# Prompt attention of a decoder step with two key-value heads on the two halves of the array

## The chip, the cores and the metric

The program runs on one core of one Trainium2 chip. It is one launch with no arithmetic on the host. The metric is the device time of a run in microseconds (us), as the median of several runs. The engines are TensorE (PE; its weight loads are PEld), VectorE (DVE), ScalarE (ACT), GpSimd (POOL) and SyncE (SP).

## The reference, cut to what matters

One layer of a decoder is applied to a prompt of 1024 tokens and to 64 sample tokens (8 sequences of 8). Everything is float32. The part that matters here is attention over the prompt. An indexer scores each key for each query, and each query keeps its best 256 keys:

```python
def _select_attend(q, qi, wi, ki_all, q_pos, gather_kv):
    ...
    score = jnp.where(admissible[None], score, -jnp.inf)
    _, sel = lax.top_k(score, topk)
    valid = sel <= q_pos[None, :, None]
    k_sel, v_sel = gather_kv(sel)
    qg = q.reshape(B, Tq, KV_HEADS, ATT_HEADS // KV_HEADS, HEAD_DIM).astype(jnp.float32)
    logits = jnp.einsum('bqhgd,bqkhd->bqhgk', qg, k_sel.astype(jnp.float32)) * (HEAD_DIM ** -0.5)
    logits = jnp.where(valid[:, :, None, None, :], logits, -jnp.inf)
    p = jax.nn.softmax(logits, axis=-1)
    o = jnp.einsum('bqhgk,bqkhd->bqhgd', p, v_sel.astype(jnp.float32))
```

There are eight query heads and four key-value heads of width 64, so two query heads share a key-value head. The other vectors that the layer needs are twelve chunks of 512 columns of an adaptive modulation, `silu(c) @ ada_w + ada_b`, for nine rows (one prompt, eight samples), and four more for the last norm.

## The kernel before, in words

The kernel runs eleven stages one after the other, with a barrier of all engines between them (`build`): modulation, projection (`norm_project`), rotary embedding, index, prompt attention, sample attention, HGRN2, output projection, routing, experts and the combination. Each stage writes out one instruction list per engine by hand. An engine takes its list in order, and waits on semaphores stand in the list. All tiles are views of one SBUF tensor (`arena`), and PSUM is eight banks (`banks`) of 128 × 512 f32.

The projection leaves all tokens in `z`, in tiles of 128 tokens: 512 query columns (eight heads of 64), 256 key columns, 256 value columns and the indexer's columns. ACT evicts each 128 × 512 result at L380; TensorE has six PSUM banks for them, so it can be ahead.

The index stage leaves, for each prompt tile i, a mask of 128 × 128(i+1) elements at `ACC_AT[i]` that is 0 for a kept key and −1e30 for another. In it DVE selects the best keys in rounds of an eight-fold maximum and a replacement (L1154 to L1158), last of all for the samples. TensorE works through projections of the recurrence and then through modulation chunks `ADA1` to `ADA2` (4 to 8), whose weights SP loads into two buffers of 2 MB (L947), one load per finished chunk. Chunks `ADA2` to `ADA3` (9 to 11) are done in prompt attention: SP loads them at L1247 to L1249, and TensorE puts one of their matmuls after each head of the first tiles (L1328, L1330).

Prompt attention goes through tiles i = 0 to 7 and the eight heads of each. Keys are transposed at L1314 into `kT`, 64 partitions per head, and queries at L1270 into `qT` (evicted by ACT at L1378). For a head, TensorE computes logits of 128 queries × 128(i+1) keys with 64 rows of the array (L1282). Two sets of two PSUM banks alternate. DVE scales them and adds the mask (L1348), and takes the row maximum in a second pass (L1351). ACT takes the exponential and its sum (L1396). TensorE transposes the result in blocks of 128 (L1294), ACT copies up to four blocks at a time back to SBUF (L1406), and TensorE multiplies each transposed block, which is the stationary operand, with 64 columns of values (L1305), accumulating in PSUM. DVE divides by the sums (L1359). In TensorE's list the transposes of head n−2 come first, then the logits of head n, then the weighing of head n−2.

In sample attention DVE reorders the 64 sample queries first (L1560). POOL's gathers of cached keys and values for the first sample are issued in prompt attention (L1210).

## Time and profile before

| what | us |
|---|---|
| three runs | 2767.02, 2760.20, 2749.53 |
| median of the runs | 2760.2 |
| the profiled execution, from its first to its last instruction | 2771.9 |
| TensorE busy | 2316.9 (84%) |
| VectorE busy | 1067.3 (39%) |
| ScalarE busy | 483.6 (17%) |
| GpSimd busy | 175.0 (6%) |

The profiled execution is one more execution beside the three that were timed; no time but its span is given for it. Busy times are sums over the whole span, and several engines are busy at once. The end of a matmul is modelled and matmuls overlap, so the time that one takes in a stream is read from the starts of two neighbours, not from its length. `banks<-arena 64*128 64x512 f32 x4` is a group of four instructions that read `arena` and write `banks`: 64 rows and 128 columns of stationary operand, and a moving operand of 64 partitions × 512 columns. `[idle <-X]` is the engine's idle time before it, and what ended it. PEclk is the clock that TensorE was granted: 1.00 is 2.4 GHz, 0.50 is 1.2 GHz.

### The profile page before, as it was taken

To read this page: it belongs to the slowest core of one execution; us is meant where nothing else is said; L and a number is where in the kernel's file an instruction comes from. 1 tells how busy PE (TensorE), PEld (TensorE's weight loads), DVE (VectorE), ACT (ScalarE), POOL (GpSimd) and SP (SyncE) were. 2 spreads that over 40 slices of the span, in tenths; PEclk is the share of its full clock that TensorE was granted. 3 is DMA by queue.
4 is the path that set the end of the run, shared out by engine and by line. 5 is a ranking of instruction groups with operands and counts; after the bars stand their busy time and mean duration, and the time that the engine had idled before them with its cause. 6 is when DMAs were issued, how large, how long until landed. Compare 5 with 4: busy or idle time off the path is not lost. (4 is left out here: it accounts for less than half of the span.)

```text
span 2771.9 us, 20892 instructions
## 1 busy us (share of the span) xinstructions
PE 2316.9 (84%) x6937; PEld 1125.3 (41%) x6938; DVE 1067.3 (39%) x2104; ACT 483.6 (17%) x832; POOL 175.0 (6%) x153
## 2 busy tenths in 40 slices
PE   5999799899991789999999579779668999999950
PEld 1444444244420346666333135435334444444420
DVE  1300469999999132222221443333411111001128
ACT  1100156210000232222111421011100000000012
POOL 0000025100000000000000000000000000000024
PEclk8999855599995575555999665589779999999985
DMA  7100210111140200001332530052178843843343
GB/s 255 58 4 0 89 45 0 46 51 66 67 143 22 100 32 1 0 1 63 137 137 92 195 112 1 4 194 91 44 274 317 314 154 141 289 165 136 136 161 112
DMA packets 117117, 294.57 MB, mean 106 GB/s; under 512 B 14862, under 2 KB 22286, under 8 KB 114483
## 3 DMA queue, kind: packets, MB, share of 16 engines
q1 hardware_dynamic: 98020, 200.90, 20.8%
q0 software_dynamic: 14272, 75.77, 7.3%
q10 hardware_dynamic: 4752, 16.93, 1.6%
q8 instruction: 46, 0.75, 0.1%
q14 instruction: 27, 0.22, 0.0%
HBM read 312.01 MB, written 44.35 MB: 129 GB/s over the span
## 5 line engine op out<-in xcount | busy, mean ns | idle before, releaser
L2066 PE MATMUL banks<-arena 128*128 x832 | 368.7, 602 | 17.2 <-DMA arena<-in_w 15.8
L1069 PE MATMUL banks<-arena 128*128 128x512 f32 (+3 forms) x656 | 255.8, 552 | 3.7 <-DMA arena<-in_ada_w 3.7
L2066 PEld LDWEIGHTS banks<-arena 128*128 128x128 f32 x832 | 159.7, 193 | 223.3 <-issue 223.3
L1154 DVE MAX8 arena<-arena 128x8 f32<-128x384 f32 (+3 forms) x224 | 238.6, 1083 | 12.9 <-DVE arena L1158 12.5
L1158 DVE MATCH_REPLACE8 arena<-arena 128x384 f32<-128x384 f32 (+3 forms) x224 | 240.7, 1075 | 0.0
L2130 DVE TENSOR_TENSOR arena<-arena,banks 128x512 f32<-128x512 f32 x26 | 17.9, 687 | 538.1 <-PE banks L2066 375.6
L364 PE MATMUL banks<-arena 128*128 128x512 f32 (+3 forms) x576 | 204.2, 515 | 0.0
L2080 PE MATMUL banks<-arena 128*128 x416 | 185.4, 599 | 11.3 <-DVE arena L2134 11.3
L1069 PEld LDWEIGHTS banks<-arena 128*128 128x128 f32 (+2 forms) x656 | 107.8, 177 | 150.8 <-issue 144.2
L1348 DVE SCALAR_TENSOR_TENSOR arena<-banks,arena 128x128 f32<-128x128 f32 (+7 forms) x64 | 48.5, 758 | 282.7 <-PE banks L1282 282.7
L1305 PEld LDWEIGHTS banks<-arena 128*128 128x128 f32 x576 | 117.0, 304 | 59.2 <-issue 38.3
L1305 PE MATMUL banks<-arena 128*128 128x64 f32 x576 | 128.3, 401 | 13.1 <-ACT arena L1406 13.1
L364 PEld LDWEIGHTS banks<-arena 128*128 128x128 f32 (+1 forms) x576 | 94.6, 186 | 104.6 <-issue 104.5
L1282 PE MATMUL banks<-arena 64*128 64x512 f32 (+3 forms) x192 | 134.9, 836 | 0.0
L1002 PE MATMUL banks<-arena 64*128 64x512 f32 (+3 forms) x192 | 127.1, 854 | 4.4 <-ACT arena L1090 2.8
L1736 PE MATMUL banks<-arena 128*128 128x512 f32 (+1 forms) x288 | 127.0, 600 | 2.8 <-DMA arena<-in_w_out 2.8
L2080 PEld LDWEIGHTS banks<-arena 128*128 128x128 f32 x416 | 77.0, 190 | 104.2 <-issue 104.2
L2107 ACT ACTIVATE arena<-banks 128x1024 f32<-128x1024 f32 x26 | 26.6, 1023 | 411.3 <-PE banks L2080 411.3
L1002 PEld LDWEIGHTS banks<-arena 64*128 64x128 f32 x192 | 58.3, 326 | 69.0 <-issue 55.7
L1396 ACT ACTIVATE arena<-arena 128x128 f32<-128x128 f32 (+7 forms) x64 | 49.4, 773 | 186.3 <-DVE arena L1351 186.2
L1736 PEld LDWEIGHTS banks<-arena 128*128 128x128 f32 (+1 forms) x288 | 53.0, 187 | 70.4 <-issue 69.8
L1282 PEld LDWEIGHTS banks<-arena 64*128 64x128 f32 x192 | 50.2, 297 | 77.2 <-issue 77.2
(352 smaller groups left out, 2485.8 us busy)
## 6 DMA issues: line engine op xcount, KB each, us to landing
arena<-in_w SPq DMA_DIRECT2D x78, 2048.0 KB
arena<-in_ada_w SPq DMA_DIRECT2D x9, 2048.0 KB, 8.5
tmp_yslot<-arena ACTq DMA_DIRECT2D x32, 512.0 KB, 2.8
arena<-in_w_in SPq DMA_DIRECT2D x7, 2048.0 KB, 8.6
arena<-in_ada_final_w SPq DMA_DIRECT2D x4, 2048.0 KB
arena<-in_ada_w SPq DMA_DIRECT2D x3, 1792.0 KB
arena<-in_x_prompt SPq DMA_DIRECT2D x1, 4096.0 KB, 25.3
arena<-in_w_out SPq DMA_DIRECT2D x2, 2048.0 KB
```

The costliest lines, as they stand in the source:

```text
L364: ins = pe.matmul(ps[0:r, n % NBK, 0:wd], hT[:, a, i * P:i * P + r], w[j % 3][:, a, 0:wd], start=(a == 0), stop=(a == KD - 1))
L1002: ins = pe.matmul(ps[:, b + c // 512, 0:w], qiT[:, h, :], kiT[:, c:c + w], start=True, stop=True)
L1069: ins = pe.matmul(ps[0:m, PB[n % 4], 0:cols], lhs(a), rhs(a), start=(a == 0), stop=(a == KD - 1 and j < len(chunks)))
L1154: ve.max(top[u][0:acc.shape[0], :], acc).then_inc(s["top"], 1)
L1158: ve.match_replace(acc, top[u][0:acc.shape[0], :], acc, TAKEN).then_inc(s["top"], 1)
L1282: ins = pe.matmul(ps[:, b + c // 512, 0:w], qT[i % 2][:, h, :], kT[:, h // 2, c:c + w], start=True, stop=True)
L1305: ins = pe.matmul(ps[:, 6 + i % 2, h * HD:(h + 1) * HD], PT[m % 4][:, u, :], z[:, c + u, VC + (h // 2) * HD:VC + (h // 2 + 1) * HD], start ...
L1348: ve.scalar_tensor_tensor(L[n % 2][:, 0:N], ps[:, b:b + 2, :].rearrange("p a b -> p (a b)")[:, 0:N], float(HD) ** -0.5, ar.view(ACC_AT[i], ...
L1396: act.activation(E[m % 2][:, 0:N], L[m % 2][:, 0:N], ACT.Exp, bias=nmx[:, m:m + 1], accum_out=den[:, m:m + 1]).then_inc(s["e"], 1)
L1736: ins = pe.matmul(ps[0:r, OUT[n % 3], :], mT[i % 2][:, a, 0:r], wo[:, a, c * 512:(c + 1) * 512], start=(a == 0), stop=(a == KD - 1))
L2066: ins = pe.matmul(ps[:, 2 + m, :], XT[b][:, a, :], w(m * 4096 + a * FE, FE), start=(a == 0), stop=(a == KD - 1))
L2080: ins = pe.matmul(ps[:, 5 + c, :], hT[:, a, :], w(8192 + a * D + c * 512, 512), start=(a == 0), stop=(a == 3))
```

## The change

Prompt attention is written anew. Tiles go from i = 7 down to 0, and each has two groups g of four query heads (two key-value heads 2g and 2g+1, two query heads r each).

- Keys and queries of two key-value heads (a = 0, 1) lie on partitions 0 to 63 and 64 to 127. Each transpose is 128 columns wide (16 for the keys, four per tile for the queries), and the logits of the two heads are matmuls on the two row halves of the array, into different banks. To make the queries of a pair neighbours, the projection's eviction of the query columns reorders heads, in two instructions of 256 columns in place of one of 512, and the sample stage's reordering reads that order.
- The scale goes into the eviction of the queries. One DVE instruction adds the mask, negates, and keeps the row minimum. ACT takes the exponential in place, with scale −1.
- The transposes are done per block c of 128 keys for the four heads of a group (four transposes into one bank). ACT copies the even blocks and DVE the odd ones.
- The values (64 columns) are the stationary operand on one column half of the array per key-value head, and 256 columns of transposed weights are moving. The output comes out transposed: DVE copies it to SBUF, TensorE turns it back, and DVE divides by the sums.
- For tiles of more than 512 keys one call of logits (r) takes all four logits banks, so it waits for the masks of the call before. TensorE's order in step n is: logits (n, 0), first half of the blocks of group n−1, logits (n, 1), second half.
- `ADA2` is 12: the three chunks of modulation are done at the end of the index stage, and SP has nothing to do in prompt attention.

The diff, with the added lines of `prompt_attention` that matter (most of the removed ones are in the listing above and are left out):

```diff
-ADA2, ADA3 = 9, 12
+ADA2, ADA3 = 12, 12
...
-                act.activation(z[0:r, i, c:c + wd], ps[0:r, n % NBK, 0:wd], ACT.Copy).then_inc(s["ev"], 1)
+                if j == 0:
+                    for g in range(2):
+                        w = slice(256 * g, 256 * g + 256)
+                        ins = act.activation(z[0:r, i, w].rearrange("p (r a d) -> p a r d", a=2, d=HD), ps[0:r, n % NBK, w].rearrange("p (a r d) -> p a r d", r=2, d=HD), ACT.Copy)
+                    ins.then_inc(s["ev"], 1)
+                else:
+                    act.activation(z[0:r, i, c:c + wd], ps[0:r, n % NBK, 0:wd], ACT.Copy).then_inc(s["ev"], 1)
...
+    A = ar.view(O_A, NT, 512)
+    kT = ar.view(O_KT, 2, SEQ)
+    PT = [ar.view(O_KT + 2 * SEQ + b * 512, 512) for b in range(4)]
...
+    LE = [ar.view(o + b * 2 * SEQ, 2, SEQ) for b in range(4)]; o += 8 * SEQ
+    qT = [ar.view(o + b * 512, 4, P) for b in range(2)]; o += 1024
...
+    order = [NT - 2 - j for j in range(NT - 1)]
+    groups = [(j, i, g) for j, i in enumerate(order) for g in range(2)]
+    base = [0]
+    for j, i, g in groups:
+        base.append(base[-1] + i + 1)
+    NG = len(groups)
+    wide = [P * (i + 1) > 512 for _, i, _ in groups]
+    def out_t(j, i):
+        return z[:, i, QC:QC + 512]
+    def halves(n):
+        i = groups[n][1]
+        return (range(0, (i + 2) // 2), range((i + 2) // 2, i + 1))
...
+            def logits(n, r):
+                j, i, g = groups[n]
+                q, N = 2 * n + r, P * (i + 1)
+                if g == 0 and r == 0:
+                    pe.wait_ge(s["ev"], j + 1)
+                first_narrow = not wide[n] and r == 0 and n > 0 and wide[n - 1]
+                if wide[n] or first_narrow:
+                    pe.wait_ge(s["l"], 2 * q)
+                elif q >= 2:
+                    pe.wait_ge(s["l"], 2 * (q - 1))
+                b = 0 if wide[n] else q % 2
                 for c in range(0, N, 512):
                     w = min(512, N - c)
+                    for a in range(2):
+                        rs = slice(HD * a, HD * a + HD)
+                        ins = pe.matmul(ps[:, 2 * a + b + c // 512, 0:w], qT[j % 2][rs, 2 * g + r, :], kT[rs, g, c:c + w], start=True, stop=True)
                 ins.then_inc(s["mm"], 1)
+            def turn(n, c):
+                m = base[n] + c
+                if c == 0:
+                    pe.wait_ge(s["e"], 4 * (n + 1))
+                if m >= 2:
+                    pe.wait_ge(s["pta"] if m % 2 == 0 else s["ptd"], m // 2)
+                for u in range(4):
+                    a, r = divmod(u, 2)
+                    ins = pe.transpose(ps[:, 4 + m % 2, u * P:(u + 1) * P], LE[(2 * n + r) % 4][:, a, c * P:(c + 1) * P], k.ident)
+                ins.then_inc(s["pt"], 1)
+            def weigh(n, c):
+                j, i, g = groups[n]
+                m = base[n] + c
+                if c == 0 and n >= 1:
+                    pe.wait_ge(s["oc"], n)
+                pe.wait_ge(s["pta"] if m % 2 == 0 else s["ptd"], m // 2 + 1)
+                for a in range(2):
+                    v0 = VC + (2 * g + a) * HD
+                    ins = pe.matmul(ps[HD * a:HD * a + HD, 6, 0:256], z[:, c, v0:v0 + HD], PT[m % 4][:, 256 * a:256 * a + 256], start=(c == 0), stop=(c == i))
                 ins.then_inc(s["pv"], 1)
+            def blocks(n, cs):
+                i = groups[n][1]
+                for c in cs:
+                    if c == 0:
+                        turn(n, 0)
+                    if c < i:
+                        turn(n, c + 1)
+                    weigh(n, c)
...
+            for b in range(4):
+                for v in range(2):
+                    for g in range(2):
+                        ins = pe.transpose(ps[:, b, (2 * v + g) * P:(2 * v + g + 1) * P], z[:, 2 * b + v, KC + g * P:KC + (g + 1) * P], k.ident)
+            pe.wait_ge(s["kc"], 4)
+            for n in range(NG + 1):
+                j, g = divmod(n, 2)
+                if g == 1 and j >= 1:
+                    turn_out(j - 1)
+                if n < NG:
+                    logits(n, 0)
+                if g == 1 and j + 1 < NT - 1:
+                    queries(j + 1)
+                if n >= 1:
+                    blocks(n - 1, halves(n - 1)[0])
+                if n < NG:
+                    logits(n, 1)
+                if n >= 1:
+                    blocks(n - 1, halves(n - 1)[1])
+            turn_out(NT - 2)
         @block.vector
...
+            def mask(n, r, a):
+                j, i, g = groups[n]
+                q, N = 2 * n + r, P * (i + 1)
+                if a == 0:
+                    ve.wait_ge(s["mm"], q + 1)
+                    if n >= 2:
+                        ve.wait_ge(s["pt"], base[n - 1])
+                b = 0 if wide[n] else q % 2
+                col = H * i + 4 * g + 2 * a + r
+                ve.tensor_tensor_reduce(LE[q % 4][:, a, 0:N], ps[:, 2 * a:2 * a + 2, :].rearrange("p a b -> p (a b)")[:, b * 512:b * 512 + N],
+                                        ar.view(ACC_AT[i], N), -1.0, 3.0e38, ALU.add, ALU.min, nmx[:, col:col + 1]).then_inc(s["l"], 1)
+            def copy_turned(n, cs):
+                for c in cs:
+                    m = base[n] + c
+                    if m % 2 == 0:
+                        continue
+                    ve.wait_ge(s["pt"], m + 1)
+                    if m >= 4:
+                        ve.wait_ge(s["pv"], m - 3)
+                    ve.tensor_copy(PT[m % 4], ps[:, 4 + m % 2, :]).then_inc(s["ptd"], 1)
+            def copy_out(n):
+                j, i, g = groups[n]
+                ve.wait_ge(s["pv"], base[n + 1])
+                ve.tensor_copy(out_t(j, i)[:, 256 * g:256 * g + 256], ps[:, 6, 0:256]).then_inc(s["oc"], 1)
+            def out(j):
+                i = order[j]
+                cols = slice(H * i, H * i + H)
+                ve.reciprocal(rden[:, cols], den[:, cols]).then_inc(s["rd"], 1)
+                ve.wait_ge(s["rd"], j + 1)
+                ve.wait_ge(s["ot"], j + 1)
+                for g in range(2):
+                    w = slice(256 * g, 256 * g + 256)
+                    ins = ve.tensor_tensor(A[:, i, w].rearrange("p (a r d) -> p a r d", r=2, d=HD), ps[:, 7, w].rearrange("p (r a d) -> p a r d", a=2, d=HD),
+                                           rden[:, H * i + 4 * g:H * i + 4 * g + 4].rearrange("p (a r) -> p a r", r=2).unsqueeze(3).broadcast_to([P, 2, 2, HD]), ALU.mult)
+                ins.then_inc(s["o"], 1)
+            for b in range(4):
+                ve.wait_ge(s["ks"], b + 1)
+                ve.tensor_copy(kT[:, :, 2 * b * P:(2 * b + 2) * P].rearrange("p g (v c) -> p g v c", c=P),
+                               ps[:, b, :].rearrange("p (v g c) -> p g v c", g=2, c=P)).then_inc(s["kc"], 1)
+            for n in range(NG + 1):
+                j, g = divmod(n, 2)
+                if g == 1 and j >= 1:
+                    out(j - 1)
+                for r in range(2):
+                    cs = halves(n - 1)[r] if n >= 1 else range(0)
+                    if n < NG:
+                        mask(n, r, 0)
+                    copy_turned(n - 1, cs[0:len(cs) // 2])
+                    if n < NG:
+                        mask(n, r, 1)
+                    copy_turned(n - 1, cs[len(cs) // 2:])
+                if n >= 1:
+                    copy_out(n - 1)
+            out(NT - 2)
         @block.scalar
...
+            def queries(j):
+                act.wait_ge(s["tr"], j + 1)
+                if j >= 2:
+                    act.wait_ge(s["mm"], 4 * (j - 1))
+                act.activation(qT[j % 2].rearrange("p a b -> p (a b)"), ps[:, 7, :], ACT.Copy, scale=float(HD) ** -0.5).then_inc(s["ev"], 1)
+            def expo(n, r):
+                j, i, g = groups[n]
+                q, N = 2 * n + r, P * (i + 1)
+                for a in range(2):
+                    col = H * i + 4 * g + 2 * a + r
+                    act.wait_ge(s["l"], 2 * q + a + 1)
+                    act.activation(LE[q % 4][:, a, 0:N], LE[q % 4][:, a, 0:N], ACT.Exp, bias=nmx[:, col:col + 1], scale=-1.0, accum_out=den[:, col:col + 1]).then_inc(s["e"], 1)
+            def copy_turned(n, cs):
+                for c in cs:
+                    m = base[n] + c
+                    if m % 2:
+                        continue
+                    act.wait_ge(s["pt"], m + 1)
+                    if m >= 4:
+                        act.wait_ge(s["pv"], m - 3)
+                    act.activation(PT[m % 4], ps[:, 4 + m % 2, :], ACT.Copy).then_inc(s["pta"], 1)
+            for n in range(NG + 1):
+                j, g = divmod(n, 2)
+                if n >= 1:
+                    expo(n - 1, 1)
+                if g == 1 and j + 1 < NT - 1:
+                    queries(j + 1)
+                if n >= 1:
+                    copy_turned(n - 1, halves(n - 1)[0])
+                if n < NG:
+                    expo(n, 0)
+                if n >= 1:
+                    copy_turned(n - 1, halves(n - 1)[1])
...
-                               .rearrange("p (c g d) -> p g c d", g=2, d=HD)).then_inc(s["qr"], 1)
+                               .rearrange("p (g c d) -> p g c d", g=2, d=HD)).then_inc(s["qr"], 1)
```

## Rows read from the trace of the kernel before

**Rows 1.** The page's head.

```profile
span 2771.9 us, 20892 instructions
```

**Rows 2.** Windows: start:end, length; per engine busy us (instructions); clock; DMA share, GB/s.

```profile
842.00:894.60 52.60, 0.00 (x0) 0.00 (x0) 50.79 (x50) 0.00 (x0) 0.00 (x0) 0.50 0.00 0
895.60:900.20 4.60, 4.58 (x22) 3.84 (x23) 2.83 (x5) 0.00 (x0) 1.88 (x2) 0.50 0.72 235
900.20:907.00 6.80, 3.33 (x25) 2.48 (x23) 3.44 (x8) 3.62 (x8) 0.00 (x0) 1.00 1.05 436
895.60:1299.60 404.00, 370.11 (x1206) 228.13 (x1206) 108.30 (x152) 108.66 (x244) 1.88 (x2) 0.57 0.07 27
1023.10:1292.70 269.60, 260.19 (x815) 176.42 (x815) 72.95 (x79) 74.19 (x148) 0.00 (x0) 0.50 0.00 0
1309.80:1347.00 37.20, 37.20 (x120) 12.42 (x119) 8.52 (x7) 5.17 (x10) 0.94 (x1) 1.00 0.23 87
```

**Rows 3.** Timeline of one head of i=7: start us, length us, instructions.

```profile
1245.73 1.92 PE L1294 MATMUL banks<-arena 128*128 128x128 f32 x8
...
1246.83 0.60 ACT L1406 ACTIVATE arena<-banks 128x512 f32<-128x512 f32 x1 [0.70 <-PE banks L1294]
...
1247.57 3.78 PE L1282 MATMUL banks<-arena 64*128 64x512 f32 x4
...
1251.28 3.67 PE L1305 MATMUL banks<-arena 128*128 128x64 f32 x16
1251.39 1.23 DVE L1348 SCALAR_TENSOR_TENSOR arena<-banks,arena 128x1024 f32<-128x1024 f32 x1 [5.71 <-PE banks L1282]
...
1253.90 1.15 ACT L1396 ACTIVATE arena<-arena 128x1024 f32<-128x1024 f32 x1 [5.63 <-DVE arena L1351]
...
1254.75 0.42 PE L1294 MATMUL banks<-arena 128*128 128x128 f32 x1
```

**Rows 4.** Groups by line within prompt attention, 895.6 to 1299.6.

```profile
L1348 DVE SCALAR_TENSOR_TENSOR arena<-banks,arena 128x128 f32<-128x128 f32 (+7 forms) x64 | 48.5, 758 | 282.7 <-PE banks L1282 282.7
...
L1328 PE MATMUL banks<-arena 128*9 128x512 f32 x48 | 35.5, 834 | 11.3 <-DMA arena<-in_ada_b 11.3
```

**Rows 5.** Timeline of TensorE in the index stage, the last two chunks of modulation.

```profile
823.42 7.04 PE L1069 MATMUL banks<-arena 128*9 128x512 f32 x16 [1.26 <-DMA arena<-in_ada_w]
...
832.46 7.04 PE L1069 MATMUL banks<-arena 128*9 128x512 f32 x16 [1.05 <-DMA arena<-in_ada_w]
```

**Rows 6.** Groups by line over the whole span, VectorE and ScalarE.

```profile
L380 ACT ACTIVATE arena<-banks 128x512 f32<-128x512 f32 (+3 forms) x36 | 18.2, 505 | 181.5 <-PE banks L364 181.5
L2134 DVE COPY arena<-banks 128x512 f32<-128x512 f32 x26 | 18.0, 691 | 19.5 <-PE banks L2072 19.5
...
L641 DVE TENSOR_TENSOR_SCAN arena<-arena 128x1088 f32<-128x1088 f32 x4 | 9.7, 2416 | 0.0
```

**Rows 7.** Timeline of the sample stage, transposes and weighing on two column halves.

```profile
1355.84 0.66 PE L1518 MATMUL banks<-arena 128*128 128x128 f32 x4
...
1356.42 2.86 PE L1534 MATMUL banks<-arena 128*64 128x256 f32 x16
...
1359.21 0.66 PE L1518 MATMUL banks<-arena 128*128 128x128 f32 x4
```

**Rows 8.** Timeline of the sample stage, two weight loads, 512-column passes.

```profile
1313.70 0.14 PEld L1497 LDWEIGHTS banks<-arena 128*64 128x64 f32 x1 [0.29 <-issue]
1314.13 0.14 PEld L1497 LDWEIGHTS banks<-arena 128*64 128x64 f32 x1 [0.29 <-issue]
```

**Rows 9.** Timeline of TensorE in the index stage, two row halves, then one.

```profile
520.96 1.97 PE L1025 MATMUL banks<-arena 64*64 64x512 f32 x4 [0.69 <-ACT arena L1100]
522.72 3.62 PE L1008 MATMUL banks<-arena 64*64 64x512 f32 x4
```

**Rows 10.** Timeline of the stage's last instructions and the next stage's first.

```profile
1295.76 2.00 PE L1305 MATMUL banks<-arena 128*128 128x64 f32 x16 [0.25 <-ACT arena L1406]
...
1299.60 0.52 SPq L1439 DMA_DIRECT2D arena<-k_rsel  x1
```

More of the change, by code:

```diff
@@ L1230, in prompt_attention @@
[L1230 to L1252 removed]
+    assert o <= O_K0, (o, O_K0)
@@ L1298, in weigh @@
-            def weigh(i, h):
-                m = first[i, h]
-                if h == 0:
-                    pe.wait_ge(s["ev"], 2 * i + 2)
-                for c in range(0, i + 1, 4):
-                    pe.wait_ge(s["ptc"], m + 1)
-                    for u in range(min(4, i + 1 - c)):
-                        ins = pe.matmul(ps[:, 6 + i % 2, h * HD:(h + 1) * HD], PT[m % 4][:, u, :], z[:, c + u, VC + (h // 2) * HD:VC + (h // 2 + 1) * HD],
-                                        start=(c + u == 0), stop=(c + u == i))
-                    m += 1
-                ins.then_inc(s["pv"], 1)
@@ new lines, in blocks, with turn_out @@
+            def blocks(n, cs):
[6 more added lines that the diff above has]
+                    weigh(n, c)
+            def turn_out(j):
+                i = order[j]
+                pe.wait_ge(s["oc"], 2 * j + 2)
+                pe.wait_ge(s["ev"], min(j + 2, NT - 1))
+                for u in range(4):
+                    ins = pe.transpose(ps[:, 7, u * P:(u + 1) * P], out_t(j, i)[:, u * P:(u + 1) * P], k.ident)
+                ins.then_inc(s["ot"], 1)
@@ L1315, in _ @@
+            for b in range(4):
+                for v in range(2):
+                    for g in range(2):
+                        ins = pe.transpose(ps[:, b, (2 * v + g) * P:(2 * v + g + 1) * P], z[:, 2 * b + v, KC + g * P:KC + (g + 1) * P], k.ident)
                 ins.then_inc(s["ks"], 1)
             queries(0)
-            pe.wait_ge(s["kc"], NT - 1)
-            for n in range(H * (NT - 1) + 2):
-                i, h = divmod(n, H)
-                if n >= 2:
-                    turn(*divmod(n - 2, H))
-                chunk, u = divmod(n - 2, ADA_EVERY)
-                if n >= 2 and chunk < len(ada) and u < KD:
-                    if u == 0:
-                        pe.wait_ge(s["aw"], 48 * (chunk + 1))
-                        if chunk:
-                            pe.wait_ge(s["ae"], chunk)
-                    pe.matmul(ps[0:NC, 1, :], k.cT[:, u, :], wa[:, u, :] if u < KD - 1 else wb, start=(u == 0), stop=False)
-                    if u == KD - 1:
-                        pe.matmul(ps[0:NC, 1, :], k.ones, bias, start=False, stop=True).then_inc(s["ap"], 1)
-                if n == 4 * H:
-                    pe.wait_ge(s["ae"], len(ada))
-                if n < H * (NT - 1):
-                    logits(i, h)
-                    if h == 4 and i + 1 < NT - 1:
-                        queries(i + 1)
-                if n >= 2:
-                    weigh(*divmod(n - 2, H))
@@ new lines, in out @@
+            def out(j):
+                i = order[j]
+                cols = slice(H * i, H * i + H)
[7 more added lines that the diff above has]
+                ins.then_inc(s["o"], 1)
```

132 lines of the change are left out of this document (10 added, 122 removed).

## The prediction

> **What bounds the kernel now.** I read the page's head first [rows 1], then busy time and granted clock in windows, because the share of the whole span (PE 84%) says nothing about one stage. Prompt attention is the stretch from 895.6 to 1299.6: 404.0 us, PE busy 370.1, DVE 108.3, ACT 108.7, clock 0.57 on average [rows 2]. So TensorE bounds it, and mostly at its lower level: from 1023.1 to 1292.7 it is busy 260.2 of 269.6 us at 0.50 (1.2 GHz) [rows 2]. Next I read the timeline of one late head (i=7) [rows 3], from start to start: eight transposes take 1.84 us (1245.73 to 1247.57), four passes of logits 3.71, sixteen passes of weighing 3.47; 9.02 us, and the next head follows without a gap. An f32 matmul is two instructions (four for the two calls of L1282, [rows 3]); a transpose is one. The logits fill 64 of the array's 128 rows and cost 0.85 us per 512 columns and pass. The weighing streams only 64 columns per pass, yet a pass takes 3.47/16 = 0.217 us, as long as a 128-column transpose (0.21): it pays for loading 128 stationary columns. Nothing here waits for DVE or ACT; DVE waits 282.7 us for logits [rows 4].
>
> **The chunks of modulation that move.** Three chunks leave the stage (PE 35.5 us busy and 11.3 us of waits, [rows 4]) for the end of the index stage. There each costs 9.04 us from start to start, its load included (823.42 to 832.46, [rows 5]), so 27 us after 841.5, until about 869. The index stage ends only with DVE's selection: from 842.0 to 894.6 PE is idle and DVE busy 50.8 of 52.6 [rows 2]. I cost them at nothing; without that cover they would be 27. Three more loads, bias loads and row stores go to SP's queue there, which nothing else needs until the barrier. In the projection nine evictions become eighteen smaller ones; ACT waited 181.5 us for PE at that line [rows 6], so nothing. The sample stage reads the same bytes in another order: nothing. POOL's gathers stay.
>
> **The new attention, at full clock.** The unit is a block: 128 keys for the four heads of a group; 2 groups × 36 = 72 blocks.
> - Transposes of a block: four, 0.58 us with the change of array mode before the next matmul (1355.84 to 1356.42, [rows 7]).
> - Weighing: two column halves, two passes each, 256 columns. Do halves overlap? In the sample stage sixteen such passes, eight on either half, take 2.79 us (1356.42 to 1359.21, [rows 7]). A 512-column pass at full clock is 0.43 (1313.70 to 1314.13, [rows 8]), so 256 columns are 0.215, and sixteen in a row would be 3.44. They overlap, though the order of issue there (eight, then eight) gives it only half a chance. Here halves alternate after two passes: 2 slots = 0.43, plus the 0.21 that 2.79 holds beyond 12 slots: 0.64. A block is 1.22 us, 72 are **87.8**.
> - Logits: row halves. In the index stage four passes on two row halves take 1.76 us at half clock (520.96 to 522.72, [rows 9]), where four on one half take 3.71 [rows 3]: full overlap. The 32 calls stream 4 × 128 × 36 = 18432 columns, 36 times 512, in two slots of 0.43: 31.0; with 0.30 per call for entering and leaving the row mode (3.71 − 4 × 0.85, [rows 3]) 9.6 more: **40.6**.
> - Queries in and outputs back: 16 sets of four transposes at 0.58, **9.3**.
>
> Is it hidden? One group of i=7 by hand: PE has two calls (4.0) and eight blocks (9.8), 13.8 us. DVE has four masks of 1.23 if the new pass costs what the masking pass costs now [rows 3], four copies of 0.69 and one of at most that [rows 6]: 8.4. ACT has four exponentials of 1.15 and four copies of 0.60 [rows 3]: 7.0, and the reads of four sums. A copy starts about 0.3 us after the last transpose, lasts 0.60 or 0.69, and PE has the weighing of the block before and the next transposes, 1.22, to cover it. It fails where DVE has just begun a mask (up to 1.2 us, about once per half group), where ACT does the last two exponentials before the next group's turn (narrow tiles), and eight times where turning the output back waits for the copy-out (0.75). I take **28** in all (6 for the last, 22 for the others), between 0 and 60. In narrow groups (i below 2) ACT's own 3 to 4 us per group hold the pace.
>
> The unseen operation is the mask with its minimum. From below it is the present masking pass, 48.5 us for 64 [rows 4]; from above two cycles per element, as the scan takes (2.42 us for 1088 elements, [rows 6]), 97. Masking and plain copies of 1024 take 1.22 to 1.23, and less is excluded, since it reads as many elements, so I take 48.5. DVE's second pass goes, which nothing waited for but ACT's exponential.
>
> Start: sixteen key transposes, copies, then three calls and two rounds of masks before the first block, because a wide tile holds all four banks of logits: 17 us, 11 beside the calls counted above. Until the clock rises these cost some **8** more. End: copy, turn, scale, barrier, **5** (now 1295.76 to 1299.60, [rows 10]).
>
> Sum: 87.8 + 40.6 + 9.3 + 28 + 11 + 8 + 5 = **190 us** against 404: 214 saved. The profiled span is 2771.9 [rows 1] and would be 2558; that execution stands 11.7 above the median of the three runs, so I put **2546**.
>
> **Does the clock rise?** It stayed at 0.50 through 269.6 us of heads with logits on one row half, PE busy 260.2. It was 1.00 after 4.6 us of nothing but key transposes at the stage's start, PE busy 4.58, and held 1.00 in the sample stage with its mix of transposes and column halves [rows 2]. With logits on both row halves, everything left resembles those. The Trainium skill, "TensorE: Matmul & The Clock Gate", Part 4 (PE-mode transpose), speaks against it: transposes don't count as activity for the clock, which would lead to the first rival below. The start of this stage disagrees: only key transposes ran, and the clock went to 1.00 [rows 2].
>
> **The rivals.**
> - *Half clock stays.* For it: the present stage. Block 0.99 + 1.11 = 2.1 × 72 = 151; logits 36 × 1.71 + 32 × 0.31 = 71; sets 16; waits 14; start 16; end 5: 273, so **2629**. Chance 0.11.
> - *Halves overlap only across their border, in strict order of issue*: two passes on the first half, two on the second make three slots, not two. Weighing 72 × 0.215 = 15.5, logits one slot per call (0.27 on average narrow, 0.43 wide) 11: **2573**. Against it: 1.76 us for four passes is two slots, not three [rows 9]. Chance 0.07. The Trainium skill, "TensorE: Matmul & The Clock Gate", Part 3 (What overlaps and what doesn't), states this strict order of matmuls; the trace disagrees, by those 1.76 us.
> - *DVE becomes the bound.* Masks at 97: DVE 97 + 24.8 (36 copies of 0.69) + 11 (16 copies out, at most 0.69) + 10 (scaling, eight times two of half a bank) + 3 (keys) + 10 (gaps) = 156, in one queue with copies that PE waits for; about 1 us more per half group, 32: **2578**. For it: each weighing waits for a copy. Chance 0.09.
> - *Halves don't overlap in this order*: 31 + 31 at full clock, **2608**; at half clock stage 396, **2752**, no change. Chance 0.04, half each.
> - *Slower: a chain through the four logits banks.* PE's next call waits for both masks, the copies stand behind masks and exponentials, and every step runs alone at half clock: blocks 72 × (1.0 + 0.95 + 1.1) = 220; 32 calls × (2.2 + 1.8 masks + 2.1 exponentials) = 195; rest 45: 460, **2816**. It decides when copies regularly stand behind an exponential whose logits PE issues after the weighing that needs the copy; the order written here puts them ahead. Chance 0.02.
>
> **How the numbers follow.** The forecast has 0.67. Its low end is no waits and full clock at once (154, 2510), with the run spread (2749.5 to 2767.0) 2505. Upwards 2610 takes in the strict order, DVE's two cycles and the serial halves at full clock; outside are half clock, the rest of serial halves, the slower case and the forecast's own tails, 0.2. A measurement tells about 1% (28 us) from no change. Faster 0.96, same 0.02, slower 0.02.
>
> **What would show it.** Stage length near 190; clock 1.00 from some 15 us after its start; masks of 1.23 for 1024; two matmuls on opposite halves starting together; index ending as before. A stage above 240 at full clock means that waits were mis-sized, at 0.50 that the clock was; an index stage that ends later means that the chunks were not covered.

## The result and the profile after

The changed kernel takes **2540.62 us** (median of four runs, 2538.1 to 2545.16), the kernel before, run beside it, 2763.61; the ratio is 0.918, with a 95% interval of 0.9134 to 0.9227. The forecast was 2546; how much of that hit is luck is said further down. The profiled execution is one of 2541.94 us with a span of 2539.8, against the span in [rows 1].

First the windows of the changed kernel. The columns are those of [rows 2]: start and end, length, busy time of PE, PEld, DVE, ACT and POOL with their instructions, mean granted clock, DMA share, GB/s. The first row is the end of the index stage, the next four are prompt attention in pieces, the last is all of it.

```profile
842.00:897.70 55.70, 45.94 (x104) 8.33 (x102) 53.82 (x55) 3.52 (x6) 0.00 (x0) 0.98 0.56 191
898.70:919.60 20.90, 15.19 (x56) 8.97 (x56) 8.76 (x14) 7.84 (x12) 1.88 (x2) 0.67 0.50 201
919.60:929.90 10.30, 9.91 (x63) 4.78 (x64) 6.19 (x10) 5.74 (x10) 0.00 (x0) 1.00 0.00 0
929.90:1059.60 129.70, 109.03 (x696) 57.52 (x692) 64.85 (x161) 59.92 (x139) 0.00 (x0) 0.99 0.00 1
1059.60:1074.90 15.30, 8.40 (x40) 4.42 (x36) 5.66 (x23) 3.12 (x13) 0.00 (x0) 0.60 0.00 1
898.70:1074.90 176.20, 142.53 (x848) 75.70 (x848) 85.46 (x208) 76.62 (x173) 1.88 (x2) 0.92 0.06 25
```

Prompt attention took 404.0 us [rows 2] and takes 176.2. That is 227.8 of the 232.1 us by which the span fell; the rest is small and of both signs. PE works 142.5 us instead of 370.1, and its clock is 0.92 on average instead of 0.57. It is 1.00 from 919.3 to 1049.0 and stands at 0.50 at times at the two ends: in the first 21 us and in the last 26, where the tiles are narrow.

The groups by line in this stretch (busy us, mean ns of one, then idle time before them and who ended it) answer to [rows 4]:

```profile
L1425 ACT ACTIVATE arena<-arena 128x1024 f32<-128x1024 f32 (+7 forms) x64 | 48.9, 767 | 17.9 <-DVE arena L1361 17.9
L1307 PE MATMUL banks<-arena 128*64 128x256 f32 x288 | 47.5, 409 | 19.8 <-DVE arena L1372 15.3 <-ACT arena L1435 4.4
L1361 DVE CUSTOM_DVE_ANT_0 arena<-banks,arena 128x1024 f32<-128x1024 f32 (+7 forms) x64 | 46.8, 754 | 59.6 <-PE banks L1285 59.6
...
L1361 DVE DVE_READ_ACCUMULATOR2_ANT arena<- 128x1 f32 x64 | 5.3, 83 | 0.0
```

L1361 is the mask with its minimum. It costs 46.8 us and 5.3 for reading the minima, so it runs at the speed of the old masking pass, 48.5 for 64 [rows 4], and not at the 97 us that the prediction had as its upper end. PE's waits in the stage, from the view of waits (total, times, longest):

```profile
PE banks L1307 <- DVE arena L1372: 15.3, 21, 1.5
PE banks L1285 <- DVE arena L1361: 4.9, 2, 2.5
PE banks L1307 <- ACT arena L1435: 4.4, 11, 0.8
PE banks L1324 <- DVE arena L1377: 4.2, 8, 0.5
PE banks L1296 <- ACT arena L1425: 2.1, 2, 1.3
```

Weighing (L1307) waits mostly for DVE's copies of transposed blocks (L1372), 21 times. The timeline of TensorE at full clock shows the unit of the sum, a block (tile i=6), and two of the waits:

```profile
939.76 0.65 PE L1307 MATMUL banks<-arena 128*64 128x256 f32 x4
940.35 0.66 PE L1296 MATMUL banks<-arena 128*128 128x128 f32 x4
941.05 0.65 PE L1307 MATMUL banks<-arena 128*64 128x256 f32 x4
941.63 0.66 PE L1296 MATMUL banks<-arena 128*128 128x128 f32 x4
942.22 0.65 PE L1307 MATMUL banks<-arena 128*64 128x256 f32 x4
943.07 0.65 PE L1307 MATMUL banks<-arena 128*64 128x256 f32 x4 [0.20 <-DVE arena L1372]
944.25 0.66 PE L1324 MATMUL banks<-arena 128*128 128x128 f32 x4 [0.53 <-DVE arena L1377]
944.84 1.77 PE L1285 MATMUL banks<-arena 64*128 64x512 f32 x8
946.54 0.66 PE L1267 MATMUL banks<-arena 128*128 128x128 f32 x4
```

From start to start: weighing 0.58 (941.05 to 941.63), transposes 0.59 (941.63 to 942.22), a block 1.17. The logits call for 896 keys takes 1.70 us (944.84 to 946.54). Its passes are two of 512 and two of 384 columns for each of two heads; one after the other, at 0.43 per 512 [rows 8], they would be 2.99.

### The profile page after: what moved, and what is told of

It is laid out like the page before. It is cut to its first block and busy times, and to the rows that moved or that the text cites. A ratio compares the mean times of both kernels' runs of the same rounds, so it can differ in the third digit from the quotient of the medians.

```text
span 2539.8 us, 20125 instructions
## 1 busy us (share of the span) xinstructions
PE 2135.9 (84%) x6633; PEld 982.0 (39%) x6634; DVE 1045.7 (41%) x2160; ACT 454.1 (18%) x773; POOL 175.4 (7%) x153
## 5 line engine op out<-in xcount | busy, mean ns | idle before, releaser
L1075 PE MATMUL banks<-arena 128*128 128x512 f32 (+3 forms) x704 | 277.0, 555 | 4.7 <-DMA arena<-in_ada_w 4.6
L2108 PEld LDWEIGHTS banks<-arena 128*128 128x128 f32 x832 | 158.5, 192 | 219.7 <-issue 219.7
L364 PE MATMUL banks<-arena 128*128 128x512 f32 (+3 forms) x576 | 203.9, 514 | 0.0
L1008 PE MATMUL banks<-arena 64*128 64x512 f32 (+3 forms) x192 | 127.1, 854 | 2.7 <-ACT arena L1088 1.5
L2122 PEld LDWEIGHTS banks<-arena 128*128 128x128 f32 x416 | 76.9, 190 | 104.4 <-issue 104.4
L1008 PEld LDWEIGHTS banks<-arena 64*128 64x128 f32 x192 | 58.2, 326 | 67.4 <-issue 54.1
L1778 PEld LDWEIGHTS banks<-arena 128*128 128x128 f32 (+1 forms) x288 | 53.1, 187 | 70.6 <-issue 70.5
L1625 DVE COPY arena<-banks 128x1024 f32<-128x1024 f32 x32 | 38.9, 1223 | 91.2 <-PE banks L1527 91.2
L1138 ACT ACTIVATE arena<-banks 128x512 f32<-128x512 f32 (+3 forms) x44 | 23.9, 544 | 265.6 <-PE banks L1075 200.2
L1361 DVE CUSTOM_DVE_ANT_0 arena<-banks,arena 128x1024 f32<-128x1024 f32 (+7 forms) x64 | 46.8, 754 | 59.6 <-PE banks L1285 59.6
L1539 PE MATMUL banks<-arena 128*64 128x512 f32 x128 | 63.0, 615 | 5.7 <-DVE arena L1625 5.7
L540 PE MATMUL banks<-arena 128*9 128x512 f32 x64 | 36.3, 730 | 36.8 <-DMA arena<-in_ada_final_w 36.8
```

What stands on the lines that cost most here:

```text
L364: ins = pe.matmul(ps[0:r, n % NBK, 0:wd], hT[:, a, i * P:i * P + r], w[j % 3][:, a, 0:wd], start=(a == 0), stop=(a == KD - 1))
L540: pe.matmul(ps[0:NC, 4 + n, :], k.cT[:, a, :], wa[n % 2][:, a, :], start=(a == 0), stop=False)
L1008: ins = pe.matmul(ps[:, b + c // 512, 0:w], qiT[:, h, :], kiT[:, c:c + w], start=True, stop=True)
L1075: ins = pe.matmul(ps[0:m, PB[n % 4], 0:cols], lhs(a), rhs(a), start=(a == 0), stop=(a == KD - 1 and j < len(chunks)))
L1361: ve.tensor_tensor_reduce(LE[q % 4][:, a, 0:N], ps[:, 2 * a:2 * a + 2, :].rearrange("p a b -> p (a b)")[:, b * 512:b * 512 + N], ar.view(A ...
L1539: pe.matmul(out, QB[:, b, pp, :], kT[(4 * b + c) % 2][:, pp, :], start=(pp == 0), stop=False)
```

## The experiments

The stage in the table is prompt attention in the profiled run, cut at its first and last instruction (403.2 us before, 175.7 changed, so cut). Where "after" stands under base, the edit is made to the changed kernel.

| kernel | base | time, us | ratio to before, 95% | stage, us |
|---|---|---|---|---|
| e1: chunks moved, nothing else | before | 2748.36 | 0.9903 to 0.9953 | 380.0 |
| e2: e1, logits on 128 rows | before | 2604.05 | 0.9383 to 0.9431 | 236.7 |
| e8: mask and minimum in one pass | before | 2771.27 | 0.9993 to 1.0034 | 414.0 |
| e3: logits on 128 rows | after | 2573.27 | 0.9274 to 0.9320 | 208.2 |
| e11: other order of passes | after | 2539.09 | 0.9118 to 0.9244 | 175.0 |
| e5: no column halves | after | 2561.83 | 0.9239 to 0.9271 | 193.1 |
| e4: two passes on DVE | after | 2586.27 | 0.9334 to 0.9364 | 220.4 |
| e6a: a copy ahead of the masks | after | 2531.24 | 0.9132 to 0.9164 | 166.1 |
| e6b: e6a, turning between halves | after | 2523.73 | 0.9099 to 0.9131 | 158.1 |
| e9: e6b, blocks in pairs | after | 2520.64 | 0.9092 to 0.9143 | 156.0 |
| e7: e6b, tile 3 first | after | 2521.88 | 0.9094 to 0.9145 | 159.1 |

**e1**: the chunks alone.

```diff
-ADA2, ADA3 = 9, 12
+ADA2, ADA3 = 12, 12
...
```

> The kernel before, with the three chunks moved to the index stage and nothing else (the heads stay one by one, on 64 rows, with two passes for mask and maximum). My theory: moving the chunks is a small part of the gain. The stage of 404 us loses their 35.5 + 4.8 + 11.3 us of TensorE work and waits, but the two stretches at a granted clock of 1.00, in which the chunks' matmuls ran beside the heads, may go with them, and at 0.50 they would cost about 44 us more: 20 to 47 us off, 2715 to 2740 us in all. Rival, that the move is what counts (the rest of the rewriting only moves work about): the stage falls towards 190, and the time below 2600 us.

The time falls by 20 us of 2768, at the small end of the 20 to 47 that were expected; 2748 itself lies above the range of 2715 to 2740. Windows of the kernel before, in the two stretches of heads that ran at 1.00, with chunks among them, then of e1:

```profile
965.00:988.90 23.90, 21.04 (x94) 9.61 (x94) 8.89 (x18) 8.97 (x26) 0.00 (x0) 1.00 0.02 3
1002.60:1023.10 20.50, 18.84 (x83) 8.65 (x82) 8.80 (x14) 6.33 (x15) 0.00 (x0) 1.00 0.00 1
```

```profile
899.60:906.40 6.80, 4.23 (x29) 3.17 (x28) 3.83 (x10) 3.69 (x9) 0.00 (x0) 0.98 1.01 434
906.40:1274.80 368.40, 349.69 (x1102) 234.52 (x1102) 101.48 (x138) 104.14 (x233) 0.00 (x0) 0.50 0.01 2
```

The stage is 23 us shorter and 368 us of it now run at 0.50. So those two stretches did go with the chunks, and the move is a tenth of the gain.

**e2**: the same, with logits that fill the array's rows. Each query is padded with zeros, so half of the multiplications are by zero.

```diff
-    kT, A = ar.view(O_KT, HKV, SEQ, p=HD), ar.view(O_A, NT, 512)
+    kT, A = ar.view(O_KT, 2, SEQ), ar.view(O_A, NT, 512)
...
-    ins = pe.matmul(ps[:, b + c // 512, 0:w], qT[i % 2][:, h, :], kT[:, h // 2, c:c + w], ...)
+    ins = pe.matmul(ps[:, b + c // 512, 0:w], qT[i % 2][:, h, :], kT[:, h // 4, c:c + w], ...)
...
```

> e1 with the logits on all 128 rows: each head's query is padded with 64 rows of zeros and meets the keys of two kv heads. The passes stay as many and as wide as in e1, nothing overlaps, and mask and maximum stay two passes. Theory A, that half of the gain is the granted clock, which stays at 0.50 while the array is fed on 64 rows: the stage runs at 1.00 and falls from about 370 to 190 to 210 us, 2540 to 2590 us in all. Theory B, that the clock rises only with what else is new (two halves at once, no gap between the steps): the clock stays at 0.50 and the time as e1's, about 2725 us.

Theory A holds: 144 us less than e1, with as many passes and columns of logits. Windows of e2, the stage in two pieces:

```profile
894.80:920.10 25.30, 18.45 (x73) 14.81 (x74) 9.99 (x34) 9.51 (x32) 1.89 (x2) 0.50 0.42 166
920.10:1131.50 211.40, 180.26 (x1065) 134.29 (x1063) 97.91 (x127) 96.72 (x225) 0.00 (x0) 0.94 0.00 1
```

It was 14 us slower than theory A's upper end. A mean of 0.94 over 211.4 us is 25 us at 0.50, and the first 25.3 us run at 0.50 too: together at most some 25 us lost to the clock, which the expectation had left out. The edit also spares the changes of mode around a call. At the 0.3 us that the prediction has for a call [rows 3] they are some 20 us for 64 calls at half clock, an estimate and a small part of the 144, and the changed kernel, which has them, runs at 1.00.

**e8**: the one pass on DVE alone.

```diff
-    ve.scalar_tensor_tensor(L[n % 2][:, 0:N], ..., ALU.mult, ALU.add).then_inc(s["l"], 1)
-    ve.wait_ge(s["l"], n + 1)
-    ve.tensor_reduce(nmx[:, n:n + 1], L[n % 2][:, 0:N], AX.X, ALU.max, negate=True).then_inc(s["mx"], 1)
+    ve.tensor_tensor_reduce(L[n % 2][:, 0:N], ..., -1.0, 3.0e38, ALU.add, ALU.min, nmx[:, n:n + 1]).then_inc(s["l"], 1)
...
```

> The kernel before, with mask and minimum in one pass on VectorE and nothing else (the chunks stay, the heads stay one by one). My theory: VectorE is not the bound, it waits 282.7 us for logits in this stage, so no change: 2755 to 2764 us. Rival, that the second pass lay in the chain from head to head: 64 reductions of 0.3 to 1.1 us go, 20 to 45 us off, 2715 to 2740 us.

No change against the kernel before in the same set of runs (2768.43), as expected, though 2771 is above the range that was written down: DVE falls from 108.3 us busy [rows 2] to 60.8 in the stage, and nothing comes of it. The stage's 414.0 in the table comes from the longest of the ten runs, in which the mean clock of the stage was 0.55, against 0.57 [rows 2].

**e3**: the changed kernel without overlap of the row halves.

```diff
-    ins = pe.matmul(..., qT[j % 2][rs, 2 * g + r, :], kT[rs, g, c:c + w], ...)
+    ins = pe.matmul(..., qT[j % 2][:, a, u * P:(u + 1) * P], kT[:, g, c:c + w], ...)
...
```

> The changed kernel with queries padded by 64 rows of zeros, so that each logits matmul has all 128 rows: the two row halves no longer run at once, everything else stays. Theory A, that passes on the two row halves overlap and save 4 slots of 0.427 us in a call of 8 passes: half of the slots come back, 72 slots of 0.427 us, +31 us, 2565 to 2578 us. Rival B, that the passes don't overlap or TensorE waits for others anyway, and what the two kv heads bring is the clock alone: 2538 to 2548 us as the changed kernel.

Theory A: 33 us slower, the stage 32.5 longer. The logits, from start to start and less their waits, take 30 us more (71.4 against 41.7), and all of PE's waits in the stage 7 more (39.2 against 31.8). A call on 1024 keys takes 3.54 us in e3 (timeline of TensorE at full clock, start to start), eight passes of 0.43 in a row:

```profile
928.17 3.70 PE L1285 MATMUL banks<-arena 128*128 128x512 f32 x8
931.71 0.60 PE L1296 MATMUL banks<-arena 128*128 128x128 f32 x4
```

**e11**: the passes of a call, sorted by head.

```diff
-    for c in range(0, N, 512):
-        for a in range(2):
+    for a in range(2):
+        for c in range(0, N, 512):
```

> The changed kernel with the passes of a logits call in another order: both column pieces of one kv head, then both of the other, instead of the two heads in turn. Nothing else is changed; all logits stay on 64 rows. Theory A, that passes on the two row halves overlap only with their neighbour in the queue, and that the clock falls when TensorE works on 64 rows for longer: of 72 saved slots some 60 come back (a call of 8 passes takes 7 slots instead of 4), 26 us at full clock, and half-clock stretches appear in the middle of the stage for 10 to 40 us more, 2571 to 2586 us. Theory B, that only the overlap is lost and the clock stays: 2563 to 2570 us. Theory C, that the halves overlap in any order: 2538 to 2546 us.

Theory C: the time is that of the changed kernel. The same call of 896 keys takes 1.71 us in e11's timeline:

```profile
931.90 1.78 PE L1285 MATMUL banks<-arena 64*128 64x512 f32 x8
933.61 0.66 PE L1296 MATMUL banks<-arena 128*128 128x128 f32 x4
```

In the trace its eight passes start in four pairs, the first at 931.90 and 931.91. So the two halves run beside each other in either order of issue, and the rival of strict order is out. The clock stays at 1.00 from 913.2 to 1049.7.

**e5**: the weighing without column halves.

```diff
-    for a in range(2):
-        v0 = VC + (2 * g + a) * HD
-        ins = pe.matmul(ps[HD * a:HD * a + HD, 6, 0:256], z[:, c, v0:v0 + HD], PT[m % 4][:, 256 * a:256 * a + 256], ...)
+    v0 = VC + 2 * g * HD
+    pe.matmul(ps[:, 6, :], z[:, c, v0:v0 + P], PT[m % 4], ...).then_inc(s["pv"], 1)
...
```

> The changed kernel without the two column halves in the weighing: the values of both heads stand on 128 columns and all 512 probability columns pass, so that half of the products are not used, and there is no change of mode between the transposes and the weighing. Theory A, that a block pays 0.30 us for its two changes of mode and saves one slot of 0.427 us by the two halves running at once: +0.13 us for each of 72 blocks, +9 us, 2546 to 2554 us. Rival B, that the changes of mode cost nothing: +0.427 us for each, +31 us, 2565 to 2577 us. Rival C, that the halves don't run at once: -0.30 us for each, 2515 to 2525 us.

The time, 21 us longer (the stage 17.4), lies between A and B. The prices hold for an undisturbed step, and the count was wrong. TensorE's timeline in e5:

```profile
937.87 1.02 PE L1306 MATMUL banks<-arena 128*128 128x512 f32 x2
938.73 0.60 PE L1296 MATMUL banks<-arena 128*128 128x128 f32 x4
...
948.83 0.60 PE L1296 MATMUL banks<-arena 128*128 128x128 f32 x4
949.26 1.02 PE L1306 MATMUL banks<-arena 128*128 128x512 f32 x2
```

Four transposes take 0.43 us here (948.83 to 949.26) and 0.585 in the changed kernel; an undisturbed weighing takes 0.86 (937.87 to 938.73) and 0.58. So a step that ends in a change of mode pays 0.15 us for it: the changed kernel's weighing is one slot of 0.43 and 0.15, where e5's is two slots, and the overlap saves 0.43. But a block doesn't have two changes within the group: the last two weighings of a group follow each other, and logits lie between the halves. In the changed kernel's trace the order of TensorE's instructions goes from transposes to weighing 58 times and back 32 times. So 72 × 0.427 − 90 × 0.15 = 17 us, close to the stage's 17.4. In part that is luck: transposes and weighing, less their waits, take 19 us more in e5 (106.3 against 87.0), and the rest of the stage is shorter, as it stood at 0.50 for 12 us in e5 and for 29 in the changed kernel.

**e4**: the changed kernel with mask and maximum in two passes.

```diff
-    ve.tensor_tensor_reduce(LE[q % 4][:, a, 0:N], ..., -1.0, 3.0e38, ALU.add, ALU.min, nmx[:, col:col + 1]).then_inc(s["l"], 1)
+    ve.scalar_tensor_tensor(LE[q % 4][:, a, 0:N], ..., ALU.mult, ALU.add).then_inc(s["l"], 1)
+    ve.wait_ge(s["l"], 2 * q + a + 1)
+    ve.tensor_reduce(nmx[:, col:col + 1], LE[q % 4][:, a, 0:N], AX.X, ALU.max, negate=True).then_inc(s["mx"], 1)
...
```

> The changed kernel with mask and maximum in two passes on VectorE again (64 reductions come back, a wait between the passes). Theory A, that VectorE, at 85.5 of 176.2 us busy but in the chain from logits to exponentials and to the copies of transposed blocks, has no room for 48 us more in one piece: a half's copies come later by up to 1.1 us, TensorE waits, +15 to +35 us, 2555 to 2576 us. Rival B, that VectorE has slack (TensorE is busy 142.5 of 176.2 us): no change, 2538 to 2546 us.

Theory A's mechanism, but 46 us, more than its upper end. Waits of e4, then two windows, the second just after a fall of the clock, and the wait in front of that fall:

```profile
PE banks L1307 <- DVE arena L1374: 36.7, 27, 3.3
PE banks L1285 <- DVE arena L1361: 7.4, 2, 3.7
```

```profile
920.90:1101.80 180.90, 137.57 (x763) 71.24 (x761) 111.85 (x177) 69.45 (x153) 0.00 (x0) 0.88 0.00 1
965.30:972.10 6.80, 5.83 (x21) 3.02 (x22) 2.29 (x4) 1.13 (x2) 0.00 (x0) 0.50 0.00 0
```

```profile
966.27 1.97 PE L1307 MATMUL banks<-arena 128*64 128x256 f32 x8 [3.27 <-DVE arena L1374]
```

PE's waits within the stage grow from 31.8 to 55.8 us, some 24 more. And the clock is 0.88 over the middle, 43 us at half speed, where the changed kernel has 3. Each of the nine falls in the middle follows a wait of 1.7 to 3.3 us; two waits of 1.8 us were followed by none. At half speed TensorE loses at most half of the added 48 us (76 against 29 over the whole stage, from the mean clocks of its windows), another 24. The two are enough for the 45 us by which the stage grew; no run here has the waits without the fall of the clock.

**e6a and e6b**: which waits of the changed kernel can go. e6a lets DVE and ACT copy the first block of a half's second half before that half's masks and exponentials; e6b moves the outputs' and the next queries' transposes, with their copies and scaling, between the halves.

```diff
+    def copies(n):
+        i = groups[n][1]
+        cut = min((i + 2) // 2 + 1, i + 1)
+        return (range(0, cut), range(cut, i + 1))
...
-                    cs = halves(n - 1)[r] if n >= 1 else range(0)
+                    cs = copies(n - 1)[r] if n >= 1 else range(0)
...
```

```diff
-                if g == 1 and j >= 1:
-                    turn_out(j - 1)
                 if n < NG:
                     logits(n, 0)
-                if g == 1 and j + 1 < NT - 1:
-                    queries(j + 1)
                 if n >= 1:
                     blocks(n - 1, halves(n - 1)[0])
+                if g == 1 and j >= 1:
+                    turn_out(j - 1)
                 if n < NG:
                     logits(n, 1)
+                if g == 1 and j + 1 < NT - 1:
+                    queries(j + 1)
...
```

> The changed kernel with the copy of the first transposed block of a half's second half moved ahead of that half's masks on VectorE (and its counterpart on ScalarE ahead of the exponentials). My theory: in the trace of the changed kernel the first block of the second half takes 1.3 to 1.74 us instead of 1.2, since its copy waits behind a mask that itself waits for the next logits: some 0.5 us in 14 groups go, -4 to -10 us, 2531 to 2537 us. Rival: the wait only moves to the next block or to the mask, and so to the exponentials: 2538 to 2546 us.

> e6a, and besides the transposes of the outputs and of the next queries moved off the ends of a group to between its two halves, on all three engines. My theory: the 8 waits of about 0.6 us before an output's transposes for the copy-out of its sum on VectorE find other work in front of them, -5 us against e6a: 2525 to 2533 us. Rival: these waits are covered by what follows or come back at the next block: as e6a, 2531 to 2537 us, or as the changed kernel.

My theory holds for both: 2531.24 us, and 2523.73, 1.3 below the range and 0.7% below the changed kernel. The stage falls by 9.6 and by 8.0 more. Waits of e6a, then of e6b:

```profile
PE banks L1312 <- DVE arena L1377: 6.0, 13, 0.9
...
PE banks L1329 <- DVE arena L1382: 4.3, 8, 0.6
```

```profile
PE banks L1312 <- DVE arena L1377: 5.4, 12, 0.9
PE banks L1290 <- DVE arena L1366: 4.9, 2, 2.5
...
PE banks L1312 <- ACT arena L1440: 4.3, 12, 0.8
PE banks L1301 <- ACT arena L1430: 3.3, 5, 1.6
```

The 15.3 us for copied blocks fall to 6.0; the eight waits before an output's transposes, 4.3 us, are gone from e6b but for one of 0.5. That is half of e6b's 8.0. The rest goes with the clock: it stood at 0.50 for 11 us of the stage in e6b and for 23 in e6a (29 in the changed kernel), most of it at the start, where the two clocks part before the first instruction that e6b moves, so I don't put it down to the edit.

**e9 and e7**, both on e6b: blocks in pairs, with the copies of two blocks instead of one ahead of a half's masks and exponentials, and tile 3 first.

```diff
+                for p in range(0, len(cs), 2):
+                    pair = cs[p:p + 2]
+                    for c in pair:
+                        if c + 2 <= i:
+                            turn(n, c + 2)
+                    for c in pair:
+                        weigh(n, c)
...
```

```diff
-    order = [NT - 2 - j for j in range(NT - 1)]
+    order = [3, 7, 6, 5, 4, 2, 1, 0]
```

> e6b with the blocks of a half taken in pairs: two blocks' transposes, then two blocks' weighings, where it was one and one. My theory: a change between transposes and weighing costs 0.15 us of TensorE (e5's rows: 0.437 and 0.861 us for the four transposes and the weighing without a change, 0.585 and 0.583 with one), and about 40 of the 90 changes inside the groups go: -6 us, -8 to -3, 2515 to 2521 us. Rival: the copies of a pair come closer together and fall behind the masks and exponentials, so that the waits of 9.7 us for copied blocks grow by as much: 2522 to 2530 us.

> e6b with another order of the query tiles: tile 3 (512 keys) first, then 7, 6, 5, 4, 2, 1, 0. My theory: the first block's transposes start 16.8 us after the stage begins, with two waits of 2.5 us for masks on 1024 keys; masks half as long and two buffers for the logits of 512 keys take these waits away and let the first block begin some 3 us earlier, also at the half clock: -1 to -6 us, 2518 to 2523 us. Rival: the wait goes to the change from 512 to 1024 keys, where the logits wait for all masks: 2523 to 2527 us.

Neither can be told from e6b by its time. In e9 transposes and weighing together take 88.3 us of TensorE's start times instead of 95.4, the 7 us that were meant, but the first logits ran longer at 0.50 (until 917.9, in e6b until 913.4) and the logits took 4.7 more. That start need not be the edit's: in e6a, too, the clock rose for good only 22.7 us after the stage's start, as in e9, and 18.8 in e6b. In e6a and e9 TensorE had stood idle for 52 us before the stage, in e6b for 4.6. In e7 the first transposes begin 11.4 us after the stage's start, in e6b 16.8 (timeline of TensorE):

```profile
896.95 3.65 PE L1335 MATMUL banks<-arena 128*128 128x128 f32 x16 [52.52 <-PEq L138]
...
908.35 1.10 PE L1301 MATMUL banks<-arena 128*128 128x128 f32 x8 [1.38 <-ACT arena L1430]
```

The stage is none the shorter for it, 159.1 against 158.1 us, so my theory falls although the time lies in its range. Part of the 5 us went into an end at 0.50, from 1049.4 on (6.7 us, in e6b 2.8); over the whole stage it stood at 0.50 for 19 us, in e6b for 11, which can cost 4 us at most. The wait that the rival named is not among TensorE's waits, and where the rest went is open.

## Why the prediction held, by its steps

The terms against the changed kernel's trace, each TensorE instruction counted from its start to the next one's, and the waits within those steps taken out where it says so:

| term | predicted | measured | from |
|---|---|---|---|
| 72 blocks | 87.8 | 87.0 | 55.6 + 51.2, less the waits in these steps: 15.6 before weighing, 4.2 before the outputs |
| logits, start, cold clock | 40.6 + 11 + 8 | 50.2 | keys 3.4, logits 53.1, less the waits 4.2 before weighing and 2.1 before transposes |
| queries and outputs | 9.3 | 11.1 | 5.6 + 5.5 |
| waits | 28 | 26.0 | 15.3 + 4.4 + 4.2 + 2.1 |
| end | 5 | 1.7 | last transposes to 1074.9 |
| sum | 190 | 176.0 | |

That the time came out 5 us from the forecast is in part luck. The span was forecast at 2558 and is 2539.8, 18 less: 14 in the stage, 4 elsewhere. From the 2558 I had taken 11.7, by which the profiled execution of the kernel before stood above the median of its runs, but the changed kernel's span is 0.8 below the median of its own. The two errors have opposite signs.

- **The clock rises**: right, and e2 shows why it was the largest step. With rows filled and little else changed from e1 (at most 20 us of mode changes), the stage falls from 380.0 to 236.7 us. The changed kernel was at 1.00 from 919.3 on, 20.6 us after its start; I had said about 15. A mix in which transposes take 45.7 of 142.5 busy us ran at 1.00 for 130 us. The Trainium skill, "TensorE: Matmul & The Clock Gate", Part 4 (PE-mode transpose), has it that transposes don't count as activity for the clock. The mix alone can't settle that, since other matmuls run in it; the start of the kernel before speaks against it, where the clock went to 1.00 after 4.58 busy us of key transposes alone [rows 2].
- **Halves overlap**: right for rows (e3, +32.5 us without it) and for columns (e5: 0.43 us per block). A block is 1.17 and not 1.22, since the weighing takes 0.58: the 0.21 that I added to two slots is one mode change, 0.15. That is 84 us for 72; the 87.0 hold some 3 more, as 6.6 us of these steps ran at 0.50. With the halves one after the other in the queue, in e11, the time is the same. The Trainium skill, "TensorE: Matmul & The Clock Gate", Part 3 (What overlaps and what doesn't), states that matmuls start and end strictly in the order of the program. e11's trace disagrees: its passes start in pairs, with four passes of one half ahead of the other's in the queue.
- **Logits**: a call for 896 keys is 1.70, of which 1.49 are slots, so a call pays 0.21 beside them, not 0.30: 3 us over 32 calls.
- **Mask with minimum at the price of a mask**: right, 754 ns against 758 [rows 4]. DVE was no bound, but had little room: e4.
- **Waits**: right in sum (26.0 against 28) and in place. e6a and e6b take 12 us of PE's waits out of the stage (31.8, then 23.7, then 19.6), and the stage falls by 17.6; how much of the rest is the clock's is open.
- **Start and end**: too dear by some 6 and 3 us. The first block's transposes come after 19 us where the terms put them at 25 (17, and 8 for the cold clock): before them the clock was already at 0.99 for 6.9 us, from 902.1 to 909.0. The last scaling ends sooner than I had it.
- **Chunks at nothing**: right, with less cover than I thought in this run. I had them end at 869; ACT's last eviction of one in the index stage starts at 891.26 and DVE's selection ends at 897.7. In e1 the last one starts at 864.95, so it isn't the chunks: TensorE's clock was 0.50 from 550 to 600 us in the changed kernel and 0.93 in e1, which is 0.43 × 50 = 22 of those 26 us. It is not the change either: e6a, e9 and e7, whose index stage is the changed kernel's, had 0.93 or 0.94 there, and their last eviction starts between 843.19 and 846.30. So it differs from run to run; why is open.

The gains don't add. The steps undone one at a time from the changed kernel cost 32.5 (row halves), 17.4 (column halves) and 45 us (one pass on DVE), and one of them alone, e8, is worth nothing in the kernel before. Between e8 and e4 lie the clock, which takes 143 us off TensorE's stage from e1 to e2, and the new order of the work; no run separates the two, so that the clock alone puts DVE's passes on the path is argued and not shown.

Of what was tried, e6b, e9 and e7 beat the changed kernel, by 0.7 to 0.8%, and can't be told from each other. Every run of theirs is shorter than each of the changed kernel's four, though these were not made beside them.

## What to carry to other kernels

Read the clock of a stage before its instruction counts: where TensorE is busy and stays at half clock on half of the rows, filling the rows, even with zeros, can be worth more than all else (143 us here, from e1 to e2). A step that another engine hides is worth nothing until the bound moves, and may then be among the dearest, so price it in the kernel that will be and not in the one that is. Count changes of array mode in the order as it is issued, not two per step of the loop.

## What the runs showed that I had not expected

- Matmuls on the two row halves run beside each other though four passes of one half stand ahead of the other's in the queue (e11: 1.71 us for a call, as with the halves in turn).
- Pauses of TensorE may cost twice: in e4, 24 us of added waits went with 48 us more at half clock, and the stage grew by 45.
- The clock of the index stage differs between runs of the same code: 0.50 from 550 to 600 us in the changed kernel and e6b, 0.93 in e6a.
- A change between transposes on the whole array and matmuls on column halves costs 0.15 us at full clock (e5: 0.585 against 0.43 for four transposes).
- A pass over 1024 elements that adds a mask, stores and takes the minimum costs what the mask alone does (mean 754 ns over the eight widths), and 83 ns for reading the minimum.
